# A two-block hybrid kernel on one core: squares summed by VectorE, one projection tile moved, filter directions on two row halves

## What is computed

```python
    a = jnp.sin(freq * (z @ w1 + b1))
    a = jnp.sin(freq * (a @ w2 + b2))
    a = jnp.sin(freq * (a @ w3 + b3))
    h = ((a @ w_out) * decay).reshape(L, N_DIRS, HYENA_ORDER, D_HYENA)
```

```python
    m = jax.nn.sigmoid(g_a) * (y_a @ w_pa[l]) + jax.nn.sigmoid(g_h) * (y_h @ w_ph[l])
    x = x + rms_norm(m @ w_out[l], post_norm[l], NORM_EPS)
```

## Time and profile before

| what | us |
|---|---|
| runs of the kernel | 2387.09, 2387.72 and 4738.23, median 2387.72 |
| profiled execution, its own time | 2388.75 |
| its span | 2386.8 |
| TensorE busy with matmuls | 2254.1 (94%) |
| VectorE busy | 1241.8 (52%) |
| ScalarE busy | 878.3 (37%) |
| GpSimd busy | 609.0 (26%) |

### The profile page before, as it was taken

How to read it: one execution, slowest core, us unless ns; L and a number is a source line. 1 busy time by engine, 2 the same in 40 slices (tenths; PEclk the granted TensorE clock), 3 DMA queues, 4 the chain that set the end, 5 groups by cost and what they waited for, 6 DMA issues and landing times.

```text
span 2386.8 us, 24783 instructions
## 1 busy us (share of the span) xinstructions
PE 2254.1 (94%) x9464; PEld 1569.7 (66%) x9464; DVE 1241.8 (52%) x1866; ACT 878.3 (37%) x1372; POOL 609.0 (26%) x282
## 2 busy tenths in 40 slices
PE   8999899998999899988989999999989899999997
PEld 4777764665677765665767876666567588756654
DVE  5677744517677744516588723332065985233321
ACT  4333254433423354333463323442135533133421
POOL 3233330333233320334332200122143321001220
PEclk9999999998999999998998998999989899989999
DMA  6313321421313221322221011112222200111221
GB/s 212 104 60 106 102 62 53 138 83 71 109 54 106 93 71 44 124 84 79 82 70 38 16 56 54 45 53 102 97 89 82 62 27 19 57 59 45 80 80 53
DMA packets 47884, 180.16 MB, mean 75 GB/s; under 512 B 5522, under 2 KB 6290, under 8 KB 46360
## 3 DMA queue, kind: packets, MB, share of 16 engines
q1 hardware_dynamic: 47672, 178.46, 23.4%
q10 hardware_dynamic: 96, 0.13, 0.0%
HBM read 163.89 MB, written 14.68 MB: 75 GB/s over the span
## 4 chain that ended last, share of the span: by engine, by line
PE 74%; DVE 21%; ACT 2%; issue 2%; DMA 1%; POOL 0%; DVEq 0%; ACTq 0%
PE bank L554 12%; PE bank L563 12%; PE bank L568 11%; PE bank L624 4%; PE bank L997 4%; PE bank L764 4%; PE bank L577 2%; PE bank L957 2%; PE bank L636 2%; PE bank L971 2%; PE bank L956 1%; PE bank L704 1%; PE bank L777 1%; DVE arena L1486 1%; PE bank L612 1%
## 5 line engine op out<-in xcount | busy, mean ns | idle before, releaser
L2046 POOL TENSOR_TENSOR w_lo<-wraw,w_hi 128x1024 fp32r<-128x1024 f32 (+1 forms) x206 | 505.4, 2454 | 1552.5 <-ACT w_hi L1019 1552.5
L1019 ACT ACTIVATE w_hi<-wraw 128x1024 fp32r<-128x1024 f32 (+1 forms) x206 | 216.6, 1051 | 779.5 <-PE bank L568 451.5
L554 PE MATMUL bank<-h_hi,w_hi 128*128 128x512 f32 x1648 | 456.8, 419 | 38.1 <-ACT h_hi L1031 30.3
L554 PEld LDWEIGHTS bank<-h_hi,w_hi 128*128 128x128 f32 x1648 | 312.7, 193 | 171.1 <-issue 84.7
L563 PE MATMUL bank<-h_lo,w_hi 128*128 128x512 f32 x1648 | 410.5, 391 | 1.0 <-POOL h_lo L2042 1.0
L568 PE MATMUL bank<-h_hi,w_lo 128*128 128x512 f32 x1584 | 391.4, 389 | 0.0
L563 PEld LDWEIGHTS bank<-h_lo,w_hi 128*128 128x128 f32 x1648 | 311.1, 189 | 69.5 <-POOL h_lo L2042 1.7
L568 PEld LDWEIGHTS bank<-h_hi,w_lo 128*128 128x128 f32 x1584 | 296.1, 187 | 63.1
L1474 DVE RECIPROCAL rs<-rs 128x512 f32<-128x512 f32 x17 | 57.0, 3353 | 171.9 <-ACT rs L1044 171.8
L624 PE MATMUL bank<-arena,wdir 128*128 128x512 f32 x256 | 114.3, 598 | 0.0
L997 PE MATMUL bank<-arena,wdir 128*128 128x512 f32 x256 | 112.4, 592 | 0.0
(11 more groups left out here) (316 smaller groups left out, 3090.9 us busy)
## 6 DMA issues: line engine op xcount, KB each, us to landing
wraw<-in_w_split SPq DMA_DIRECT2D x204, 512.0 KB, 3.5
wdir<-in_w_direct SPq DMA_DIRECT2D x60, 512.0 KB, 3.6
x_park<-arena SPq DMA_DIRECT2D x3, 2048.0 KB, 6.3
arena<-x_park SPq DMA_DIRECT2D x3, 2048.0 KB, 8.0
hg_park<-arena SPq DMA_DIRECT2D x2, 2048.0 KB, 9.4
arena<-hg_park SPq DMA_DIRECT2D x2, 2048.0 KB, 8.3
arena<-bias_rows SPq DMA_DIRECT2D x2, 1792.0 KB, 7.3
arena<-in_xT SPq DMA_DIRECT2D x2, 1024.0 KB, 7.2
```

The source lines that it names most:

```text
L554: mm(ps[0:wd, 0:S], hi[:, k, :].bitcast(F32R), h_hi[:, k, :].bitcast(F32R), start=k == 0 and not begun, stop=False)
L1019: a(w_hi[:, n % 2, 0:f].bitcast(F32R), wraw[:, n % 2, 0:f], ACT.Copy).then_inc(hi_done, 1)
L2046: nc.gpsimd.tensor_tensor(w_lo[:, n % 2, 0:f].bitcast(F32R), wraw[:, n % 2, 0:f], w_hi[:, n % 2, 0:f], ALU.subtract).then_inc(lo_done, 1)
```

## The change

Three parts. First, `add_squares` on VectorE adds the 8 squared tiles into the first of them, as they come, and the column sum is one matmul. This is done for "ps" of both layers and "ss" of B1 and F. At "ps" ScalarE squares from the bank, ahead of the copy, and for the last tile ahead of the weight split too. Second, tile v2 moves from `(1, "ut")` to the front of `(1, "us")`, on TensorE, ScalarE and in the order of banks and weights. Third, the last network layer gets doubled columns, so that its result stands twice, on rows 0 to 63 and on rows 64 to 127 of `aT`; the output weights `fwo` hold direction 0 on the first rows and direction 1 on the others, and each direction's matmul uses its own half. Tables on the host are laid out for it.

```diff
-    (0, "iy"): [("v", 1)], (1, "ut"): [("v", 2)],
-    (1, "us"): [("v", 3)] + [("za", j) for j in range(4)] + [("zh", 0), ("zh", 1)],
+    (0, "iy"): [("v", 1)], (1, "ut"): [],
+    (1, "us"): [("v", 2), ("v", 3)] + [("za", j) for j in range(4)] + [("zh", 0), ("zh", 1)],
...
-        mlpw = sb("mlpw", [FW, 3, FW])
-        mlpc = sb("mlpc", [FW, 4])
+        mlpw = sb("mlpw", [FW, 2 * FW + DIRS * FW])
+        mlpc = sb("mlpc", [DIRS * FW, 4])
...
-                        mm(ps[0:FW, 0:S], mlpw[:, n, :], aT[0:FW, :], start=True, stop=True).then_inc(filled("mlp", l, n), 1)
+                        span_ = FW * (DIRS if n == 2 else 1)
+                        mm(ps[0:span_, 0:S], mlpw[:, n * FW:n * FW + span_], aT[0:FW, :], start=True, stop=True).then_inc(filled("mlp", l, n), 1)
...
-                        mm(ps[:, 0:512], aT[0:FW, tb:S:RES],
-                           fwo[:, d, :], start=True, stop=True).then_inc(filled("flt", l, o, tb, d), 1)
+                        rows_ = slice(FW * d, FW * d + FW)
+                        mm(ps[:, 0:512], aT[rows_, tb:S:RES],
+                           fwo[rows_, :], start=True, stop=True).then_inc(filled("flt", l, o, tb, d), 1)
...
-                column_sums(("ps", l), [(hs["A0"][:, k, :], ("post_sq", l, k)) for k in range(KT)])
+                column_sums(("ps", l), [(hs["A0"][:, 0, :], ("post_acc", l))])
...
-                column_sums(("ss", ph), [(hs[ph][:, k, :], ("sq", ph, k)) for k in range(KT)])
+                column_sums(("ss", ph), [(hs[ph][:, k, :], ("sq", ph, k)) for k in range(KT)] if l == 0 else
+                            [(hs[ph][:, 0, :], ("sq_acc", 0))])
...
-            column_sums(("ss", "F"), [(hs["F"][:, k, :], ("sq", "F", k)) for k in range(KT)])
+            column_sums(("ss", "F"), [(hs["F"][:, 0, :], ("sq_acc", 1))])
...
-                    await_split("wo", l, j)
+                    if j == KT - 1:
+                        act.wait_ge(*full("wo", l, j))
+                    else:
+                        await_split("wo", l, j)
+                    a(hs["A0"][:, j, :], bank("wo", l, j)[:, 0:S], ACT.Square).then_inc(up("post_sq", l, j), 1)
+                    if j == KT - 1:
+                        await_split("wo", l, j)
                     a(PH[:, j, :], bank("wo", l, j)[:, 0:S], ACT.Copy).then_inc(release("wo", l, j), 1)
                     act.wait_ge(*read("wo", l, j))
-                    a(hs["A0"][:, j, :], PH[:, j, :], ACT.Square).then_inc(up("post_sq", l, j), 1)
...
+            def add_squares(tiles, which, squares, done, l):
+
+                for k in which:
+                    dve.wait_ge(*after(*squares, k))
+                    if k:
+                        ins = v.tensor_tensor(tiles[:, 0, :], tiles[:, 0, :], tiles[:, k, :], ALU.add)
+                        if k == KT - 1:
+                            ins.then_inc(up(done, l), 1)
+                        else:
+                            link(ins)
...
                 lo_odd(f"M{l}", PA)
+                add_squares(hs["A0"], range(KT), ("post_sq", l), "post_acc", l)
...
                     dve.wait_ge(*read("wo2", l, k))
+                    if k:
+                        add_squares(hs["F"], (k - 1,), ("sq", "F" if l else "B1"), "sq_acc", l)
+                add_squares(hs["F"], (KT - 1,), ("sq", "F" if l else "B1"), "sq_acc", l)
```

More of the change, by code:

```diff
@@ L204 @@
 STEPS = {
-    "ones": (), "sel": (), "gc_rows": (DEPTH,), "beta_rows": (DEPTH,), "relb": (H,), "sq": (5, KT), "h": (5, KT), "h_hi": (8, KT), "h_lo": (8, KT // 2), "h_lo_odd": (8, KT // 2),
+    "post_acc": (DEPTH,), "sq_acc": (DEPTH,), "ones": (), "sel": (), "gc_rows": (DEPTH,), "beta_rows": (DEPTH,), "relb": (H,), "sq": (5, KT), "h": (5, KT), "h_hi": (8, KT), "h_lo": (8, KT // 2), "h_lo_odd": (8, KT // 2),
     "post": (DEPTH, KT), "x": (DEPTH, KT // 2), "x_odd": (DEPTH, KT // 2),
@@ L253, in program @@
         banks = [ctx.enter_context(nc.psum_tensor(f"bank{i}", [P, 512], F32)) for i in range(8)]
-        ARENA = 31488
+        ARENA = 31360
         with nc.sbuf_tensor("arena", [P, ARENA], F32) as arena:
@@ L278, in program @@
         rh = region([("_", HYENA), ("pq", 4096), ("HG", 4096), ("uN", 2048), ("UV", 2048), ("ot", 1024),
-                     ("fwo", 1024), ("aT", 512)])
+                     ("fwo", 512), ("aT", 512)])
         rt = region([("_", HYENA), ("bias", H * SPAN), ("o", 2048), ("L", 2048), ("WT", 4096),
@@ L293, in program @@
         fls = (fl, uN)
-        fwo = arena[0:FW, rh["fwo"]:rh["fwo"] + DIRS * S].rearrange("p (d n) -> p d n", d=DIRS)
+        fwo = view(rh, "fwo", S)
         ztab = arena[0:EMB, rh["uN"]:rh["uN"] + S]
@@ L462, in _ @@
                         sp.wait_ge(*after("ya", n - 1, H - 1))
-                    for dst, src in ((mlpw[0:EMB, 0, :], t["w1"][n]), (mlpw[:, 1, :], t["w2"][n]),
-                                     (mlpw[:, 2, :], t["w3"][n]), (mlpc[:, :], t["mlpc"][n]),
+                    for dst, src in ((mlpw[0:EMB, 0:FW], t["w1"][n]), (mlpw[:, FW:2 * FW], t["w2"][n]),
+                                     (mlpw[:, 2 * FW:], t["w3"][n]), (mlpc[:, :], t["mlpc"][n]),
                                      (lamv[:, :, :], t["lamv"][n].partition_broadcast(P))):
@@ L468, in _ @@
                     sp.dma_start(delta, t["deltas"][n][FILTER_OF[0]].partition_broadcast(P)).then_inc(delta_in, 16)
-                    sp.dma_start(fwo, t["flt_w_out"][n][:, :, FILTER_OF[0], :]).then_inc(delta_in, 16)
+                    sp.dma_start(fwo, t["flt_w_out"][n][:, FILTER_OF[0], :]).then_inc(delta_in, 16)
                 elif kind == "transforms":
@@ L477, in _ @@
                     sp.wait_ge(*full("flt", n, 0, 3, 1))
-                    sp.dma_start(fwo, t["flt_w_out"][n][:, :, FILTER_OF[1], :]).then_inc(delta_in, 16)
+                    sp.dma_start(fwo, t["flt_w_out"][n][:, FILTER_OF[1], :]).then_inc(delta_in, 16)
                     sp.wait_ge(*after("decay", n, 0, 3))
@@ L602, in network @@
                         pe.wait_ge(ztab_in, 16 * (l + 1))
-                        mm(ps[0:FW, 0:S], mlpw[0:EMB, 0, :], ztab, start=True, stop=True).then_inc(filled("mlp", l, n), 1)
+                        mm(ps[0:FW, 0:S], mlpw[0:EMB, 0:FW], ztab, start=True, stop=True).then_inc(filled("mlp", l, n), 1)
                     else:
                         pe.wait_ge(*after("mlp_sb", l, n - 1))
-                        mm(ps[0:FW, 0:S], mlpw[:, n, :], aT[0:FW, :], start=True, stop=True).then_inc(filled("mlp", l, n), 1)
+                        span_ = FW * (DIRS if n == 2 else 1)
+                        mm(ps[0:span_, 0:S], mlpw[:, n * FW:n * FW + span_], aT[0:FW, :], start=True, stop=True).then_inc(filled("mlp", l, n), 1)
                 def filters(o, tb):
@@ L1104, in _ @@
                         act.wait_ge(*after("mlp_arg", l, j // 2))
-                        a(aT[0:FW, :], aT[0:FW, :], ACT.Sin).then_inc(up("mlp_sb", l, j // 2), 1)
+                        span_ = FW * (DIRS if j == 4 else 1)
+                        a(aT[0:span_, :], aT[0:span_, :], ACT.Sin).then_inc(up("mlp_sb", l, j // 2), 1)
                     if j == 5:
@@ L1503, in mlp_arg @@
                     dve.wait_ge(*full("mlp", l, n))
-                    arg, k_ = tmp[0:FW, 0, :], tmp[0:FW, 1, :]
-                    v.tensor_scalar(arg, bank("mlp", l, n)[0:FW, 0:S], mlpc[:, n:n + 1], mlpc[:, 3:4],
+                    span_ = FW * (DIRS if n == 2 else 1)
+                    arg, k_ = tmp[0:span_, 0, :], tmp[0:span_, 1, :]
+                    v.tensor_scalar(arg, bank("mlp", l, n)[0:span_, 0:S], mlpc[0:span_, n:n + 1], mlpc[0:span_, 3:4],
                                              ALU.add, ALU.mult).then_inc(release("mlp", l, n), 1)
@@ L2171 @@
         "lamv": np.stack([x[n] for n in ("lam_q1", "lam_k1", "lam_q2", "lam_k2")], 1),
-        "w1": x["flt_w1"], "w2": x["flt_w2"], "w3": x["flt_w3"],
-        "mlpc": np.stack([x[n] for n in ("flt_b1", "flt_b2", "flt_b3", "flt_freq")], -1),
-        "flt_w_out": x["flt_w_out"].reshape(DEPTH, FW, DIRS, ORDERS, 512),
+        "w1": x["flt_w1"], "w2": x["flt_w2"], "w3": np.concatenate([x["flt_w3"]] * DIRS, -1),
+        "mlpc": np.concatenate([np.stack([x[n] for n in ("flt_b1", "flt_b2", "flt_b3", "flt_freq")], -1)] * DIRS, 1),
+        "flt_w_out": x["flt_w_out"].reshape(DEPTH, FW, DIRS, ORDERS, 512).transpose(0, 2, 1, 3, 4).reshape(
+            DEPTH, DIRS * FW, ORDERS, 512),
         "deltas": x["flt_deltas"].reshape(DEPTH, DIRS, ORDERS, 512).transpose(0, 2, 1, 3),
```

2 lines of the change are left out of this document (1 added, 1 removed).

## The result

The changed kernel took 2359.78 us (median of 4 runs, 2352.18 to 2360.91), the kernel before 2391.16 (median of the 4 runs beside it), a ratio of 0.9868 with an interval of 0.9834 to 0.9901: 31 us less. Forecast were 28.8 us and 2359. One run of before, at 4738.23, is a disturbed one and stays out of the ratio; the median of the other three (2387.09, 2387.72 and 2394.60) is 2387.72, and against that the changed kernel is 28 us faster. The profiled execution took 2360.57 (span 2358.5, mean granted clock 0.957), 28.2 less than the 2388.75 of before.

A forecast was written before the change was run, and what follows sets the result against it. TensorE was taken as the main bound, with 74% of the chain that ended last. Filters 13.8, tile 5.6 and squares 9.4 sum to 28.8 us off the median 2387.72, giving 2358.9, stated as 2359; range 2350 to 2370.

The forecast's parts named there:

- Filters: Filter stage: matmuls on two row halves overlap, saving 1.72 us in each of 8 groups, 13.8 in all.
- Rival A: Filter stage: weight loads of the two row halves run in turn, saving 7.2 us, total 2365.5; chance 0.12.
- Rival C: Filter stage: VectorE's sums become the bound, so the filter gain is lost, total 2372.7; chance 0.07.
- the room after the change: Filter stage: VectorE's last sum moves about 4 us forward, leaving some 5 before TensorE needs it.
- Tile: Convolution 2: moving tile v2 saves 2.8 us a layer, 5.6 for both.
- The new wait: Convolution 2, before the signal transform: TensorE waits 2.3 us for ScalarE's copies, costing 1.7 in clock.
- Rival B: The new 2.3 us wait costs no clock and the table load stays hidden, total 2354.5; chance 0.20.
- Squares: Four column sums at "ps", B1 and F: VectorE adds squares, one matmul remains, saving 9.4 us.
- the table load behind the sum: Root at "ps": two waits put the square-root table load of 1.28 us on the path.
- the add beside GpSimd: B1: VectorE's last add meets GpSimd's subtraction, takes 2.43 us instead of 0.71; the site gains 0.7.
- The lone sum at F: F: a chance of half clock for the single matmul costs 0.4 us, leaving 2.9 of 3.3.
- Rival D: Long half-clock stretches in dense work behind six new or earlier waits make it slower, 2397.5; chance 0.03.

The follow-up runs named there:

- e1: Kernel before with only the filter part (two row halves, doubled third network layer): 2381.53 us, ratio 0.9946.
- e2: Kernel before with only tile v2 moved: 2385.98 us, ratio 0.9967.
- e8: Changed kernel with the fourth-block turning of convolution 2 issued four times, filling TensorE's wait: 2352.20 us, ratio to before 0.9826.
- e3: Kernel before with only the four column sums changed: 2375.07 us, ratio 0.9925.
- e7: Changed kernel with a one-column square root ahead of the root's wait at the four sums, loading the table early: 2353.87 us, ratio to before 0.9836.
- e6: Changed kernel with the last square of wo2 ahead of ScalarE's weight split: 2355.07 us, ratio to before 0.9841.
- e11: Kernel before with only the sums at B1 and F changed, "ps" as before: 2390.54 us, ratio 0.9995.
- e4: The changed kernel timed again, beside the single parts: 2354.95 us, ratio to before 0.9840.
- e9: Changed kernel with three small edits (last square first, table loaded early, repeated turning in the wait): 2347.75 us, ratio to before 0.9822.
- e10: Kernel before with only the two "ps" sums changed, B1 and F as before: 2378.75 us, ratio 0.9946.

## Why the prediction was right

- **Filters, 13.8:** right. 13.1 in the profile of e1, 12.9 by its ratio. Rival A (loads in turn, 7.2) is out, since a group takes 2.11 and its loads run two at a time. Rival C is out, since TensorE never waited on VectorE's sums. But the step that gave the room after the change was wrong: I counted VectorE's last sum as moving 4 forward and some 5 of room left, and e1 shows it moving 0.7 (1.3 without what the start of the kernel lost) and 2.3 left. The count followed the tiles and left GpSimd out, which rows 13 would have told me to look for.
- **Tile, 5.6:** right, with each of its steps. The new wait was put at 2.3 and is 2.28. What it costs in clock was put at 1.7 and is 1.65 to 1.80. In layer 0 of e2 the inverse starts 1.08 earlier, forecast 0.95, and at full clock it takes 1.87 less, forecast 1.8. Sum 2.95, forecast 2.8. e8 shows that the wait is the cause of the clock loss. Rival B's half of this (no clock cost) is out.
- **Squares, 9.4 at the sites:** 8.2 in e3. "ps" was put at 2.9 each and gave 2.44 and 2.79, B1 at 0.7 and gave 0.48, F at 2.9 and gave 2.46. Both places that were argued from mechanism, the table load behind the sum and the add beside GpSimd, are as forecast, and e7 and e6 take each of them away. The lone sum at F runs at half clock in the changed kernel (1.84), which I had weighed at 0.4 and which costs 0.8. In e11 it had the full clock (1.15), and F gained 3.3.
- **What the sum left out:** 6 to 10 us of clock in layer 0's latent attention, which came with the "ps" part. It is a term that the sum had at nothing. The prediction looked for clock only directly behind the edited places. It also took one execution for the kernel before. That execution was 6 us fast in just this stretch (404.8 where four others had 410.9 to 411.0), which made the profiled difference, 28.2, look like the forecast.
- **Rival D**, time lost to long half-clock stretches behind the new waits, is out. Behind the two new waits before L645 they are 3.4 long. Behind the lone sums there are long ones (13.7 at 519.9, 23.9 at 1697.5), but TensorE has little to do there (it is busy for 5.3 of those 13.7), and little is lost: from the reciprocal of "ps" to the one of the next norm it is 18.06 before and after, and behind B1 it is 40.00 where it was 39.66. Rival D counted them in dense work.
- That the median of 2359.78 lies on the forecast is in part luck. The forecast starts from 2387.72 for the kernel before, 4 to 6 below its medians in the other groups (2392.12 to 2393.24), and the surplus makes up for that. e4's 2354.95 is the same kernel and lies 4 below the forecast, inside the range of 2350 to 2370; as a saving it is 38.3, a third more than 28.8.

## What to carry to other kernels

Where a chain of small steps ends a phase, look at what else the same engine would do in that gap: moving one square ahead of a weight split, loading a table before the wait and filling a wait of 2.3 with repeated work gave 7 us together (e9 against e4, in two groups of runs), nearly as much as the sums did at their sites. Check the room of an engine that you pass by after your change as well as before it, with its collisions. And time the parts of a change alone, more than once: one profile differs from the next of the same kernel by as much as a part is worth.

## What was not expected of the hardware

- A wait does not have a fixed price in clock. The same 1.11 before the same matmuls is followed by 10.2 us at 1.2 GHz in one kernel and by none in another (e11, e10). It differs between two executions of the kernel before, too. With an edit 430 us upstream the bad case is in none of nine profiles, without the edit in four of five.
- A weight load with a stride of 4 takes 305 ns also on alternating row halves, and 8 passes still end in 2.11. Before, on one half, a group's eight loads took 305 each too; now the two halves' loads run side by side, eight in 1.40.
- At the four sums looked at, the load of the square-root table went ahead of the wait where one wait stood before the root ("ps" before), and behind it where two did (B1 and F, and "ps" after the change). A one-column square root ahead of the waits brings it forward for 0.20.
